# Attention units in another order, w_out's rows to match, and a second buffer for the norm's root

## What is computed

```python
gla_o  = merge_heads(rms_norm(chunked_gated_linear_attention(gq, gk, gv, gla_log_a), gla_norm_w))     # 4 heads of 256
hgrn_o = merge_heads(rms_norm(chunked_gated_linear_attention(hq, hgrn_k, hi, hgrn_log_f), hgrn_norm_w)) # 4 heads of 128
p  = softmax(xq @ mk.T * XATTN_HEAD_DIM ** -0.5)
xo = merge_heads(rms_norm(p @ mv, xattn_norm_w))                                                       # 4 heads of 128, keys from mem
mixed = concatenate([gla_o, hgrn_o, xo]) * silu(gate)                                                  # 256 x 2048
x = rms_norm(x + mixed @ w_out, final_norm_w)
```

## Times and profile before

| | us |
|---|---|
| median of 3 runs | 1087.94 (1087.07 to 1089.46) |
| the profiled execution's own time | 1087.07 |
| its span in the profile | 1085.3 |
| PE busy in the span | 1023.1 (94%) |
| POOL, DVE, ACT busy | 762.6, 549.1, 468.7 |
| mean granted TensorE clock | 0.97 of full speed |

### The profile page before, as it was taken

How to read it: one execution, slowest core, us unless ns; L and a number is a source line. 1 busy time by engine, 2 the same in 40 slices (tenths; PEclk the granted TensorE clock), 3 DMA queues, 4 the chain that set the end, 5 groups by cost and what they waited for, 6 DMA issues and landing times.

```text
span 1085.3 us, 21538 instructions
## 1 busy us (share of the span) xinstructions
PE 1023.1 (94%) x8142; PEld 995.9 (92%) x8142; DVE 549.1 (51%) x1020; ACT 468.7 (43%) x698; POOL 762.6 (70%) x599
## 2 busy tenths in 40 slices
PE   7999999989899999998999899989999889999996
PEld 6899899989899999997898789989999879999995
DVE  4316994455444443335695463445654764445324
ACT  6243224454355444434546434423235364444441
POOL 2496666647859888996578734646629739999994
PEclk9999999999989999998999899989999889999998
DMA  9363333433526555664353122434225526656662
GB/s 351 106 194 117 117 117 117 136 98 117 194 82 184 173 181 159 181 178 152 117 169 107 57 62 94 120 115 126 90 79 172 188 69 194 193 179 185 178 182 70
DMA packets 48297, 154.60 MB, mean 142 GB/s; under 512 B 6028, under 2 KB 11156, under 8 KB 48232
## 3 DMA queue, kind: packets, MB, share of 16 engines
q1 hardware_dynamic: 46080, 151.31, 44.6%
q10 hardware_dynamic: 2152, 2.38, 0.6%
HBM read 151.57 MB, written 2.10 MB: 142 GB/s over the span
## 4 chain that ended last, share of the span: by engine, by line
PE 76%; DVE 12%; issue 4%; POOL 4%; ACT 3%; DMA 0%; SPq 0%; DVEq 0%; ACTq 0%; POOLq 0%
PE panel L1517 59%; PE panel L1561 3%; POOL wlo L591 2%; PE aux L1653 1%; PE panel L1604 1%; DVE qkv L1246 1%; DVE qkv L1251 1%; PE panel L1592 1%; DVE q L1154 1%; DVE s L1133 1%; DVE qkv L1242 1%; DVE k L1155 1%; PE aux L1875 1%; PE aux L1847 1%; PE aux L1838 1%
## 5 line engine op out<-in xcount | busy, mean ns | idle before, releaser
L591 POOL TENSOR_TENSOR wlo<-raw,whi 128x512 fp32r<-128x512 f32 x552 | 733.5, 1360 | 301.2 <-ACT whi L679 299.9
L1517 PE MATMUL panel<-xh,whi 128*128 128x256 f32 (+1 forms) x1504 | 443.5, 295 | 14.5 <-DVE xl L985 9.9
L1517 PE MATMUL panel<-xh,wlo 128*128 128x256 f32 (+1 forms) x1504 | 431.3, 287 | 0.0
L1517 PE MATMUL panel<-xl,whi 128*128 128x256 f32 (+1 forms) x1504 | 430.7, 286 | 0.0
L679 ACT ACTIVATE whi<-raw 128x1024 fp32r<-128x1024 f32 x276 | 286.5, 1053 | 175.0 <-PE panel L1517 152.2
L1517 PEld LDWEIGHTS panel<-xh,whi 128*128 128x128 f32 x1504 | 288.3, 192 | 19.3 <-issue 11.5
L1517 PEld LDWEIGHTS panel<-xl,whi 128*128 128x128 f32 x1504 | 287.4, 191 | 1.6
L1517 PEld LDWEIGHTS panel<-xh,wlo 128*128 128x128 f32 x1504 | 288.0, 191 | 0.0
L1517 PE MATMUL panel<-hh,whi 128*128 128x272 f32 (+1 forms) x352 | 100.1, 284 | 0.0
L1517 PE MATMUL panel<-hh,wlo 128*128 128x272 f32 (+1 forms) x352 | 99.9, 284 | 0.0
L1517 PE MATMUL panel<-hl,whi 128*128 128x272 f32 (+1 forms) x352 | 99.8, 284 | 0.0
(11 more groups left out here) (285 smaller groups left out, 1495.0 us busy)
## 6 DMA issues: line engine op xcount, KB each, us to landing
raw<-in_panels SPq DMA_DIRECT2D x228, 512.0 KB, 3.5
raw<-in_down SPq DMA_DIRECT2D x32, 448.0 KB, 3.3
raw<-in_down SPq DMA_DIRECT2D x16, 512.0 KB, 3.5
memk<-in_mem_panels SPq DMA_DIRECT2D x4, 512.0 KB, 7.4
memv<-in_mem_panels SPq DMA_DIRECT2D x4, 512.0 KB, 13.2
memx<-in_mem SPq DMA_DIRECT2D x4, 256.0 KB, 5.2
h<-in_x SPq DMA_DIRECT2D x1, 1024.0 KB, 8.0
spill<-h ACTq DMA_DIRECT2D x1, 1024.0 KB, 4.7
```

The source lines that it names most:

```text
L591: ins = nc.gpsimd.tensor_tensor(wlo[:, slot, half], raw[:, slot, half], whi[:, slot, half].bitcast(f32), ALU.subtract)
L1517: ins = M(bank[:, 0:w], wt[:, slot, P * t:P * t + P], x[:, kk, c0:c0 + w], start=first and m == 0 and n == 0, stop=last and m == len(pairs ...
```

## The change

`UNITS = (6, 0, 7, 1, 2, 3, 4, 5)` is the order in which the units are now taken: step i works on unit `UNITS[i]`. A memory pair goes first, then a GLA head, the other memory pair, the other heads. In the list of steps, the value pair of V+4 and V+5 now comes ahead of the first unit, and two units follow each value pair; the norm of a unit is set after the next unit's products as before, sometimes with a value pair between. Four units are done by the time of the first panel of `w_out`, so its first halves now hold the rows of units 6, 0, 7 and 1: the host reorders `w_out` and PE reads the mix tiles by `MIX_TILES`. The root has two buffers, `rstd` and a second one in the place of `prob`, and ACT waits for the gate product two units back. DVE also waits for `mix_low` before it reuses an `ot` buffer.

```diff
@@ -47,6 +47,8 @@
 
 
 XQ, GATE, V = 16, 20, 36
+UNITS = (6, 0, 7, 1, 2, 3, 4, 5)
+MIX_TILES = [2 * u + e for u in UNITS for e in range(2)]
 
 
 def first_schedule():
@@ -62,12 +64,14 @@
     for u in (0, 2):
         steps += [("scores", u), ("scores", u + 1), ("weights", u), ("weights", u + 1)]
         steps += [("out", V + u), ("out", V + u + 1), ("probs", u), ("probs", u + 1)]
-    for q in range(10):
-        steps += [("out", V + 2 + 2 * q), ("out", V + 3 + 2 * q)] if 1 <= q < 5 else []
-        steps += [("o", q)] if q < 8 else []
-        steps += [("o_norm", q - 1)] if 1 <= q < 9 else []
-        steps += [("o_split", q - 2)] if q >= 2 else []
-        steps += [("wout", q - 6)] if q >= 6 else []
+    def v_panels(n):
+        return [("out", V + 2 * n), ("out", V + 2 * n + 1)]
+
+    steps += v_panels(2) + [("o", 0), ("o", 1)] + v_panels(3) + [("o_norm", 0), ("o", 2), ("o_norm", 1), ("o_split", 0)]
+    steps += v_panels(4) + [("o", 3), ("o_norm", 2), ("o_split", 1), ("o", 4), ("o_norm", 3), ("o_split", 2)]
+    steps += v_panels(5) + [("o", 5), ("o_norm", 4), ("o_split", 3), ("o", 6), ("wout", 0), ("o_norm", 5), ("o_split", 4)]
+    steps += [("o", 7), ("wout", 1), ("o_norm", 6), ("o_split", 5), ("o_norm", 7), ("wout", 2), ("o_split", 6), ("wout", 3)]
+    steps += [("o_split", 7)]
     return steps
 
 
@@ -310,6 +314,7 @@
         gate = at("gate", ar + 17408, [P, 16, ROWS])
         ot = at("ot", ar + 21504, [P, 4, 2, ROWS])
         prob = at("prob", ar + 23552, [P, 2, 2, ROWS])
+        orstd = rstd, at("rstd_odd", ar + 23552, [P, 512])
         glr = at("glr", ar + 24576, [16, ROWS])
         small1 = at("small1", ar + 24832, [P, 64])
         pt = at("pt", tmp_at, [P, 4, 2, ROWS])
@@ -790,14 +795,17 @@
                     A(sqo[:, i % 4], ot[:, i % 4], ACT.Square).then_inc(o_squared, 1)
                 if kind == "o_norm":
                     bank, n = aux("o_norm", i)
-                    w, count = (ROWS, 256.0) if i < 4 else (2 * ROWS, 128.0)
+                    w, count = (ROWS, 256.0) if UNITS[i] < 4 else (2 * ROWS, 128.0)
                     aux_wait(act, n)
+                    if i > 1:
+                        act.wait_ge(o_mixed, i - 1)
                     if i:
-                        act.wait_ge(o_mixed, i)
-                    root(bank, n, w, count, rstd).then_inc(o_rstd, 1)
+                        act.wait_ge(o_rstd, i)
+                    root(bank, n, w, count, orstd[i % 2]).then_inc(o_rstd, 1)
                 if kind == "o_split":
                     act.wait_ge(o_mixed, i + 1)
-                    A(mixh[:, 2 * i:2 * i + 2, :], ot[:, i % 4], ACT.Copy).then_inc(mix_high, 1)
+                    u = UNITS[i]
+                    A(mixh[:, 2 * u:2 * u + 2, :], ot[:, i % 4], ACT.Copy).then_inc(mix_high, 1)
             for m in range(4, 16):
                 ahead(WOUT_P + m)
 
@@ -1178,19 +1186,22 @@
                     bank, n = aux("o", i)
                     if i >= 4:
                         dve.wait_ge(mix_high, i - 3)
+                        dve.wait_ge(mix_low, i - 3)
                     aux_wait(dve, n)
                     CP(ot[:, i % 4].rearrange("p e r -> p (e r)"), bank[:, :]).then_inc(aux_free[n % 4], 1)
                 if kind == "o_norm":
+                    u = UNITS[i]
                     dve.wait_ge(o_rstd, i + 1)
                     for e in range(2):
-                        wv = vcol("gla_norm", e) if i < 4 else vcol("hgrn_norm" if i < 6 else "xattn_norm")
-                        r = rstd[:, 0:ROWS] if i < 4 else rstd[:, ROWS * e:ROWS * e + ROWS]
+                        wv = vcol("gla_norm", e) if u < 4 else vcol("hgrn_norm" if u < 6 else "xattn_norm")
+                        r = orstd[i % 2][:, 0:ROWS] if u < 4 else orstd[i % 2][:, ROWS * e:ROWS * e + ROWS]
                         ins = STT(ot[:, i % 4, e, :], ot[:, i % 4, e, :], wv, r, ALU.mult, ALU.mult)
                     order(ins)
-                    TT(ot[:, i % 4], ot[:, i % 4], gate[:, 2 * i:2 * i + 2, :], ALU.mult).then_inc(o_mixed, 1)
+                    TT(ot[:, i % 4], ot[:, i % 4], gate[:, 2 * u:2 * u + 2, :], ALU.mult).then_inc(o_mixed, 1)
                 if kind == "o_split":
                     dve.wait_ge(mix_high, i + 1)
-                    TT(mixl[:, 2 * i:2 * i + 2, :], ot[:, i % 4], mixh[:, 2 * i:2 * i + 2, :].bitcast(f32),
+                    u = UNITS[i]
+                    TT(mixl[:, 2 * u:2 * u + 2, :], ot[:, i % 4], mixh[:, 2 * u:2 * u + 2, :].bitcast(f32),
                        ALU.subtract).then_inc(mix_low, 1)
             take_in(WOUT_O, 2)
             dve.wait_ge(rstd_ready, 3)
@@ -1576,7 +1587,7 @@
                 pe.wait_ge(lo_ready, p + 1)
                 if half == 0:
                     pe.wait_ge(bank_free[o % 4], o // 4)
-                products(pb[o % 4], p % RING, [(t, 8 * half + t) for t in range(8)], mixh, mixl, 0, ROWS,
+                products(pb[o % 4], p % RING, [(t, MIX_TILES[8 * half + t]) for t in range(8)], mixh, mixl, 0, ROWS,
                          half == 0, half == 1).then_inc(passed, 1)
 
 
@@ -1677,30 +1688,31 @@
                         .then_inc(aux_full, 1)
                 if kind == "o":
                     bank, n = aux("o", i)
+                    u = UNITS[i]
                     aux_open(n)
-                    if i == 0:
+                    if u == 0:
                         for g in range(2):
                             for l in (6, 7, 8):
                                 for x in range(2 if l < 8 else 1):
                                     aux_freed(pe, AUX[("level", l, g, x)])
-                    if i == 6:
-                        for u in range(4):
-                            aux_freed(pe, AUX[("probs", u)])
+                    if u == 6:
+                        for n_ in range(4):
+                            aux_freed(pe, AUX[("probs", n_)])
                         for o in range(4, 8):
                             bank_freed(pe, o)
-                    if i < 6:
-                        bank_freed(pe, IN_O + V + 2 * i)
-                        bank_freed(pe, IN_O + V + 2 * i + 1)
+                    if u < 6:
+                        bank_freed(pe, IN_O + V + 2 * u)
+                        bank_freed(pe, IN_O + V + 2 * u + 1)
                     for e in range(2):
-                        if i < 6:
-                            hd = i if i < 4 else 2 * i - 4 + e
-                            col = P * (2 * i + e)
+                        if u < 6:
+                            hd = u if u < 4 else 2 * u - 4 + e
+                            col = P * (2 * u + e)
                             M(bank[:, ROWS * e:ROWS * e + P], v[:, 0, col:col + P], s[:, hd, 0:P], start=True, stop=True)
                             M(bank[:, ROWS * e + P:ROWS * e + ROWS], v[:, 0, col:col + P], s3[:, hd, :], start=True, stop=False)
                             ins = M(bank[:, ROWS * e + P:ROWS * e + ROWS], v[:, 1, col:col + P], s[:, hd, P:ROWS],
                                     start=False, stop=True)
                         else:
-                            hd = 2 * (i - 6) + e
+                            hd = 2 * (u - 6) + e
                             for mt in range(2):
                                 ins = M(bank[:, ROWS * e:ROWS * e + ROWS], mv[:, mt, P * hd:P * hd + P], pt[:, hd, mt, :],
                                         start=mt == 0, stop=mt == 1)
@@ -1710,7 +1722,7 @@
                     aux_open(n)
                     pe.wait_ge(o_squared, i + 1)
                     for e in range(2):
-                        if i < 4:
+                        if UNITS[i] < 4:
                             ins = M(bank[:, 0:ROWS], ones[:], sqo[:, i % 4, e, :], start=e == 0, stop=e == 1)
                         else:
                             ins = M(bank[:, ROWS * e:ROWS * e + ROWS], ones[:], sqo[:, i % 4, e, :], start=True, stop=True)
@@ -2039,7 +2051,7 @@
             by_step[("gate", b, i)] = gates[8 * b + i]
             by_step[("branch", b, i)] = p[i // 2]
     mixer = [by_step[step] for step, (_, _, half) in MIX_OUT.items() if not half]
-    w_out = pack(x["w_out"], 16).reshape(8, P, 2, 1024)
+    w_out = pack(x["w_out"], 16).reshape(8, P, 16, P)[:, :, MIX_TILES, :].reshape(8, P, 2, 1024)
     w_out = np.stack([w_out[i, :, half] for i, half in W_OUT])
     panels = np.concatenate([pack(p, KT) for p in (hf, gk, gq, hq, xq, gate, gv, hi)]
                             + [w_out, up(x["ffn1_wi_2"]), np.stack(mixer), pack(x["w_out_2"], KT), up(x["ffn2_wi_2"])])
```

## The result

The changed kernel takes 1092.75 us (median of 5 runs, 1091.49 to 1093.37), the kernel before 1087.07 us (5 runs, 1086.77 to 1089.46): ratio 1.005, 95% interval 1.0037 to 1.0063. It is slower by 5.7 us. All ratios in this text are of fast executions; three far slower ones of the later comparisons (one each of e3, e6 and the kernel before) are left out. Its profiled execution took 1092.24 us with a span of 1090.4 us, 5.1 us longer than the span before.

What follows compares the result with a forecast made beforehand. PE, busy 94% of the span, bounds the kernel; only stops or low clock could be won. Fifth panel +3.85 us and low clock +2.4 us make +6.25 us, 1093.3 us, forecast as 1094.0 us; range set 1086.5 to 1098.0.

Steps and rivals of the forecast that it cites:

- PE's position at the first `w_out` panel and the first stop: PE arrives at 236.1 us, waits 4.9 us for `mixl` delayed by collisions with POOL, goes on at 241.0 us.
- The walk: Pass through the new list of steps with the profiled durations, charging DVE's collisions with POOL; total +6.25 us.
- The value pair ahead: Value pair moved ahead of the first unit: PE waits 0.4 us for POOL's subtraction; nothing won.
- The clock behind the first stop: First `w_out` panel runs at 1.2 GHz after the stop and takes 5.4 us; low clock priced at 2.6 us.
- The stretch to the fifth panel: Step 6's product by the root at 254.2 us to PE at 263.9: 5.2 us path plus five collisions, 4.5 us.
- The clock behind the second stop: Clock falls again after the 5.3 us stop, costing 2.4 to 2.6 us over the fifth and sixth panel.
- Two root buffers: Second buffer for the root: only the last root gains, up to 1.13 us; nothing at the other steps.
- Sum: Fifth panel +3.85 us later plus low clock +2.4 us: total +6.25 us, forecast 1094.0 us; chance 0.62.
- (a): Whole-instruction blocking: each of eight DVE-POOL collisions costs some 0.2 us more, +1.6 us, 1095.6 us; chance 0.12.
- (b): POOL's halves fall into DVE's waits for ACT; stops 2.6 and about 1 us, clock stays up, 1083 us; chance 0.14.
- (c): Clock falls only once: second stop 3 us, three collisions fewer, +1.2 us, 1089.1 us; chance 0.10.
- (d): Root's second buffer lets units follow at DVE's pace of 2.1 us; nearly all 8.0 us won, 1080 us; chance 0.02.

Runs made afterwards that it cites:

- e3: Changed kernel, complete, with ACT's splits of the third, fifth, sixth and later `w_out` panels moved in its queue; ratio to the kernel before 0.9972.
- e6: Kernel before with 20 idle matmuls on PE ahead of the first `w_out` panel; ratio to the kernel before 0.9991.
- e1: Changed kernel with POOL's subtractions of the second to seventh `w_out` panel cut to an eighth of their columns, the rest left out; ratio to before 0.9978.
- e7: New order of units, matching `w_out` rows and two root buffers, in the old list of steps; ratio to the kernel before 1.0035.
- e4: Changed kernel with one root buffer and the old wait for the gate product of the unit before; ratio to the kernel before 1.0047.
- e2: Kernel before with POOL's subtractions of six `w_out` panels cut to an eighth of their columns, the rest left out; ratio to before 0.9991.
- e10: Kernel before with ACT's splits moved: the fifth `w_out` panel's ahead of the eighth unit's square, later ones' behind the last `mixh`; ratio to before 0.9978.
- e8: New list of steps and two root buffers with the units in their old order; ratio to the kernel before 1.0060.
- e11: The changed kernel measured again, nothing altered, beside later runs on the same chip; ratio to the kernel before 1.0064.

## Why the prediction was right, point by point

- *PE's position at the first `w_out` panel and the first stop.* The walk said 241.0 us and 4.9 us; the trace has 241.12 us and 4.55 us idle. The splits came at 232.66 us (said: 232.6 and 233.6), POOL worked from 233.8 to 239.5 us (said: 239.3), the two products by the root began at 237.24 us (said: 237.2). PE came to the panel 0.5 us later than the walk had it, so the stop is shorter though it ends later. e1 and e3 leave the collision of step 2 where it is (the walk charged 0.9 us for it, the trace has 1.86 us for a pair of 0.88) and have a stop of 2.9 us; the walk's 2.6 us was for no collision at all. The collision of step 4 cost 1.6 us for the 1.4 of the walk. One more pair, at 216.25 us, took 1.99 us; the walk did not see it, and it cost nothing, since the copy of step 3 then waited for PE.
- *The value pair ahead.* 0.39 us for 0.4. But "nothing is won by it" was wrong: with a memory pair first, it covers a stop of 1.54 us (e7).
- *The clock behind the first stop.* Mis-sized: 1.8 us (4.63 against 2.84), where the walk had 2.6. The stop was longer than before and the first panel's loss shorter, so the old price could not be carried over.
- *The stretch to the fifth panel.* Said 254.2 to 263.9 us with five collisions, 4.5 us; it ran from 253.38 to 263.47 us. The collisions cost 4.6 us by e1, and the path without them 5.5 us, where the walk had 5.2. It began 0.8 us earlier than said, by the clock's missing 0.8 us, and ended 0.4 us earlier.
- *The clock behind the second stop.* 2.4 us for 2.4.
- *Two root buffers.* Said to gain up to 1.13 us at the last root. That step failed: without it e4 took 0.9 us less from step 6's product to PE, because the start that the buffer makes possible, 1.0 us earlier, met POOL.
- *Sum.* +5.1 us in the span, for +6.25. Of the difference, 0.4 us are in the position of the fifth panel; the rest is at the next stop, at the end of the first block, where the clock was low while PE worked for 5.0 us before and for 3.4 us after by the windows of 296 to 310 us: 0.8 us given back at half speed. The forecast of 1094.0 us also carried over 0.7 us by which the median before lay above its profiled execution; in the comparison the median before was 1087.07 us, the same as that execution, and the changed kernel measured 1092.75 us. That the sum is this close is in part luck: its price of the low clock was 0.8 us too high, its last path to PE 0.3 us too short, its arrival of PE 0.5 us too early, and it left out what the next stop would give back; some of these cancel. The mechanism is not luck: both stops, the splits, POOL's halves and the slow products stand where the walk put them.

Of the rivals, (a), blocking for the whole instruction, would have put the fifth panel at 265.5 us. The pair at 237.24 us speaks against it too: the first product began 0.81 us before the end of POOL's half and took 1.09 us, 0.6 more than the 0.48 us of one alone; the second began 1.19 us before the end of the next half and took 1.48 us, 1.0 more. So some 0.2 us of each rest of a half were not paid for, as the walk had it from the row at 209.58 us (the ends of POOL's operations are rough in a profile). (b), the collisions miss, is what e3 then made true by moving the splits: the stage fell by 9.5 us, where it said 11, and e3 is 3 us faster than the kernel before, where it said 5. (c) and (d) did not happen: the clock fell twice, and with either number of root buffers the steps follow each other at the same pace but for the last (e4).

One reason behind the prediction needs mending. It took the fall of the clock as a consequence of the stops' length. e2 has the stops of the kernel before to 0.01 us without a fall, and e10 had one with the same two stops; e1 (2.92 us) had one and e3 (2.93 us) had none; e6 had one behind 1.80 us, and e8 none behind 2.23 and 2.43 us. Only the stops of over 4 us had one each time here (two in the changed kernel, two in e11, one in e8, two in e4). So the 2.6 us that the prediction wanted to win back were not there in each execution of the kernel before, and e6 could gain only in those where it fell.

## What to carry over

Where two engines can't work at once, a list of steps has to be judged by when the background engine works, not by how its work is counted. Here the same subtractions cost some 8 us more or less, by the place of four splits in ACT's queue, and two quite different orders of the attention units took the same time, as far as the runs can tell, once those splits were placed. Walk the chain that releases the bound engine with the durations of the rows, mark on it where the background work falls, and move that first. A step that starts earlier is no gain by itself: it may start into the other engine's turn.

## What the runs showed of the hardware

- The length of a stop of 2 to 3 us did not tell here whether the granted clock fell behind it: with stops equal to 0.01 us it fell in two executions (before, e10) and stayed at 1.00 in another (e2); a stop of 2.92 us had a fall (e1) and one of 2.93 us had none (e3); one of 1.80 us had a fall (e6). After a fall the first panel took 5.49 us in the kernel before and 4.63 us in the changed one, behind a longer stop. What decides it, no run here shows.
- In these traces a vector operation with two SBUF inputs and a POOL subtraction of 128 x 512 take turns: of two products by the root at 237.24 us, one waited out what was left of POOL's half (1.09 us) and the next nearly a whole one (1.48 us), 1.6 us over the 0.88 us for both without POOL. POOL pays as well: its half at 238.01 us took 1.44 us, the one before 1.26 us. The copies out of PSUM in these timelines keep their 0.69 us beside POOL (before, at 231.03 us).
